# Twelve load slots and one form of matmul per product in the experts of a first layer

## What is computed

```python
def expert_choice_ffn(h, router, w_gate, w_up, w_down):
    cap = CAPACITY_FACTOR * t // N_EXPERTS            # 64 of 512 tokens, 32 of 256 context rows
    aff = softmax(h @ router)
    gates, idx = lax.top_k(swapaxes(aff, 1, 2), cap)  # 16 experts
    xs = h[idx]
    a = einsum('becd,edf->becf', xs, w_gate)          # 1024 x 1024 per expert
    u = einsum('becd,edf->becf', xs, w_up)
    y = einsum('becf,efd->becd', silu(a) * u, w_down)
    return zeros.at[idx].add(y * gates)

x_new = x_new + g2 * expert_choice_ffn(h2, ...)
if need_ctx:                                          # first layer only
    xc = xc + cg2 * expert_choice_ffn(hc2, ...)
```

## Time and profile before

| | us |
|---|---|
| median of 3 runs (2745.11 to 2752.82) | 2745.65 |
| the profiled execution | 2749.64 |
| its span from first to last instruction | 2747.8 |
| granted TensorE clock, mean of the span | 0.973 |

### The profile page before, as it was taken

How to read it: one execution, slowest core, us unless ns; L and a number is a source line. 1 busy time by engine, 2 the same in 40 slices (tenths; PEclk the granted TensorE clock), 3 DMA queues, 4 the chain that set the end, 5 groups by cost and what they waited for, 6 DMA issues and landing times.

```text
span 2747.8 us, 35463 instructions
## 1 busy us (share of the span) xinstructions
PE 2540.7 (92%) x13952; PEld 1520.0 (55%) x13952; DVE 1313.6 (48%) x2565; ACT 1002.7 (36%) x1859; POOL 355.3 (13%) x190
## 2 busy tenths in 40 slices
PE   6999988899999998796869999998899898999998
PEld 3875566432222322684654433442667787788887
DVE  2497544344444444577542333333754654442342
ACT  4216642244344443526523222222344334322222
POOL 0220002001111111220010000000223221122221
PEclk9999999899999999999989999999999899999999
DMA  6216733599999998320039999998121002222221
GB/s 255 66 62 241 281 123 123 218 359 375 365 355 371 370 361 332 127 92 1 16 146 372 421 421 421 421 421 352 47 77 32 15 13 96 94 92 98 92 85 54
DMA packets 85452, 567.72 MB, mean 207 GB/s; under 512 B 11744, under 2 KB 12000, under 8 KB 20264
## 3 DMA queue, kind: packets, MB, share of 16 engines
q1 hardware_dynamic: 79128, 547.01, 51.0%
q0 software_dynamic: 3616, 11.80, 1.9%
q10 hardware_dynamic: 2544, 6.66, 0.7%
HBM read 550.74 MB, written 14.68 MB: 206 GB/s over the span
## 4 chain that ended last, share of the span: by engine, by line
PE 46%; DVE 3%; DMA 1%; ACT 1%; issue 1%; ACTq 0%; DVEq 0%
PE PS L1024 11%; PE PS L1124 4%; PE PS L1122 4%; PE PS L1123 4%; PE PS L1136 3%; PE PS L1137 3%; PE PS L1138 3%; PE PS L1082 2%; PE PS L1112 2%; PE PS L795 1%; PE PS L1248 1%; DMA X<-in_w_up_dram 1%; PE PS L1253 1%; PE PS L1168 1%; PE PS L1154 1%
## 5 line engine op out<-in xcount | busy, mean ns | idle before, releaser
L2646 POOL TENSOR_TENSOR WHL<-RING,WHL 128x1024 fp32r<-128x1024 f32 x64 | 172.7, 2698 | 1489.4 <-ACT WHL L1369 1489.4
L1024 PE MATMUL PS<-RING,RF 128*64 128x512 f32 x1208 | 284.6, 603 | 4.0 <-DVE AR L2303 1.4
L1024 PE MATMUL PS<-WIDE,RF 128*64 128x512 f32 x1168 | 269.5, 597 | 0.0
L1369 ACT ACTIVATE WHL<-RING 128x1024 fp32r<-128x1024 f32 x129 | 134.5, 1047 | 213.1 <-PE PS L1138 129.4
L1122 PE MATMUL PS<-RR,WHL 128*128 128x512 f32 x512 | 205.0, 400 | 1.8 <-DVE RR L2399 1.8
L1124 PE MATMUL PS<-RR,WHL 128*128 128x512 f32 x512 | 203.2, 397 | 0.0
L1123 PE MATMUL PS<-RR,WHL 128*128 128x512 f32 x512 | 201.6, 394 | 0.0
L1024 PEld LDWEIGHTS PS<-RING,RF 128*64 128x64 f32 x1208 | 78.9, 137 | 181.6 <-issue 172.7
L1024 PEld LDWEIGHTS PS<-WIDE,RF 128*64 128x64 f32 x1168 | 79.2, 136 | 166.8 <-issue 155.5
L1877 DVE TENSOR_TENSOR WHL<-RING,WHL 128x1024 fp32r<-128x1024 f32 x65 | 79.5, 1224 | 172.3 <-ACT WHL L1369 166.1
L1624 ACT ACTIVATE RF<-PS,MODS,MSC 128x128 f32<-128x128 f32 x192 | 74.4, 438 | 231.0 <-PE PS L1082 129.9
(11 more groups left out here) (386 smaller groups left out, 4931.5 us busy)
## 6 DMA issues: line engine op xcount, KB each, us to landing
RING<-in_w_gate_dram SPq DMA_DIRECT2D x75, 1024.0 KB, 7.5
WIDE<-in_w_down_dram SPq DMA_DIRECT2D x69, 1024.0 KB, 7.8
RING<-in_w_up_dram SPq DMA_DIRECT2D x61, 1024.0 KB, 5.7
RING<-in_ada_w_dram SPq DMA_DIRECT2D x48, 1024.0 KB, 6.4
WIDE<-in_w_up_dram SPq DMA_DIRECT2D x45, 1024.0 KB, 8.3
RING<-in_w_down_dram SPq DMA_DIRECT2D x38, 1024.0 KB, 8.1
WIDE<-in_w_gate_dram SPq DMA_DIRECT2D x32, 1024.0 KB, 8.8
RING<-in_w_in_dram SPq DMA_DIRECT2D x30, 1024.0 KB, 5.0
```

The costliest lines, as they stand in the source:

```text
L1024: ins = e.matmul(a[r:r + 64, :], xs[:, j, 0:64], w[:, i, :], start=j < 2, stop=j > 5)
L1369: e.activation(h, load_buffer(ld)[:, js, cs], ACT.Copy).then_inc(act, A(("hi", st["i"])))
L2646: e.tensor_tensor(lo, load_buffer(loads[st["load"]])[:, js, cs], h.bitcast(F32), ALU.subtract).then_inc(pool, G(("lo", st["i"])))
```

## The change

In the first layer's experts twelve slots take the place of six. Added are slot 3, a part of RF (slot 8), two parts of AR that held HN (9 and 11), and the two pairs of token tiles of X (12 and 13). The rows of X and HN are written to DRAM ahead of slot 3's first load in that layer, and slots that lie in X, AR or RF wait for what was there before. `product` on TensorE now takes both loads of a product: one form on both in the first half, the other form on both in the second, and the form changes its place from product to product, so that a product begins with the form in which the one before ended. A product's two loads are released in its second half. In the first layer the pump runs twice in the first half of a product and not in the second, where it ran once in each; between `index` and the first `pick` lie eight pumps in place of four. One scratch buffer moves from RF to AR. The second layer keeps its order.

```diff
-                wide = len(loads) - 4
+                wide = len(loads) - (4 if l else 5)
         for ld in loads[wide:]:
-            ld["slots"] = (7, 8, 9, 4, 5, 6, 10, 0, 1, 2, 3) if l else (4, 5, 6, 0, 1, 2)
-        for ld in loads[wide - 4:]:
+            ld["slots"] = (7, 8, 9, 4, 5, 6, 10, 0, 1, 2, 3) if l else (4, 5, 6, 8, 3, 12, 13, 9, 11, 1, 2, 0)
+        for ld in loads[wide - (4 if l else 3):]:
             ld["expert"] = True
...
-                wide = st["i"] if k in (4, 5, 6) else wide
+                wide = st["i"] if k in (4, 5, 6) or "expert" in ld and layer == 0 else wide
...
-    next(ld for ld in loads if "expert" in ld and ld["before"] and "expert" in ld["before"])["rows"] = True
-    next(ld for ld in loads if ld["slot"] == NRING)["sums"] = True
+    next(ld for ld in loads if ld["slot"] == NRING)["rows"] = True
+    next(ld for ld in loads if ld["slot"] == NRING and ld["lead"][0])["sums"] = True
...
             plan.append(("index", g))
-            for _ in range(4):
+            for _ in range(8):
                 yield
...
-        for _ in range(1 if need_ctx else (0, 2)[q]):
+        for _ in range((2, 0)[q] if need_ctx else (0, 2)[q]):
             pump()
...
-        CD, CE = [rf(8704, 512), rf(9216, 512)], [rf(9728, 512), rf(10240, 512)]
+        CD, CE = [rf(8704, 512), rf(9216, 512)], [rf(9728, 512), ar(10688, 512)]
...
+                if "fresh" in ld:
+                    layer = ld["fresh"]
+                    if layer == 0 and ld["slot"] in (3, 12, 13):
+                        e.wait_ge(sums_out, 16 * 6)
+                    elif layer == 0 and ld["slot"] in (9, 11):
+                        e.wait_ge(rows_out, 16 * 6)
+                        e.wait_ge(pe, P["pick", 0, 0, 7])
+                    elif layer == 0:
+                        e.wait_ge(pe, P["pv", 0, 47])
...
+                def product(a, b, xs, q, *names):
+
+                    if q == 0:
+                        pair.clear()
+                        turn.append(tokens if len(turn) % 2 or not need_ctx else context)
+                        for n in range(2 if need_ctx else 1):
+                            pair.append(weights())
+                            st, w, _ = pair[n]
+                            ins = turn[-1](a if turn[-1] is tokens else b, xs, st, w, n == 0, n == 1)
+                        if not need_ctx:
+                            ins.then_inc(pe, P(("w", st["i"])))
+                    elif need_ctx:
+                        other = context if turn[-1] is tokens else tokens
+                        for n in (1, 0):
+                            st, w, _ = pair[n]
+                            other(a if other is tokens else b, xs, st, w, n == 1, n == 0
+                                  ).then_inc(pe, P(("w", st["i"]), *(names if n == 0 else ())))
```

More of the change, by code:

```diff
@@ L181, in weight_steps @@
     q, last_q, nq, wide, split = -1, {}, 0, None, None
+    layer, fresh = None, set()
     for ld in loads:
@@ L186, in weight_steps @@
         ld.update(slot=k, n=count[k], before=last.get(k), after=split if k in (4, 5, 6, 10) else None)
+        layer = ld["lead"][0] if "expert" in ld else layer
+        if k >= NRING and (k, layer) not in fresh and not k in (4, 5, 6, 10):
+            fresh.add((k, layer))
+            ld["fresh"] = layer
         last[k] = ld
@@ L573, in program @@
         rows_in, mask_in, bias_in = sem("rows_in"), sem("mask_in"), [sem(f"bias_in{i}") for i in range(2)]
-        weights_in = [sem(f"weights_in{i}") for i in range(NRING + 8)]
+        weights_in = [sem(f"weights_in{i}") for i in range(NRING + 11)]
         P, A, V, G = Done(pe), Done(act), Done(dve), Done(pool)
@@ L606, in landing @@
             else:
-                b = (rf(8192, 2048), rf(10240, 2048), ar(4096, 2048), rf(6144, 2048))[ld["slot"] - NRING - 4]
+                b = (rf(8192, 2048), rf(10240, 2048), ar(4096, 2048), rf(6144, 2048), ar(2048, 2048),
+                     *(X[:, t:t + 2, :].rearrange("p a b -> p (a b)") for t in (0, 2)))[ld["slot"] - NRING - 4]
             return b[:, 0:ld["nj"] * ld["cw"]]
@@ L745, in sync @@
                         e.dma_start(X[:, t, :], XROWS[128 * t:128 * t + 128, :]).then_inc(sums_in[t], 16)
+                    e.wait_ge(dve, V["hn", "1a", 5])
                 if "scratch" in ld:
@@ L757, in sync @@
                             e.wait_ge(dve, V["lo", st["i"]])
[L758 to L761, removed]
+                if "fresh" in ld:
[7 more added lines that the diff above has]
+                        e.wait_ge(pe, P["pv", 0, 47])
+                    elif ld["slot"] != NRING:
+                        e.wait_ge(pe, P["pv", 1, 31])
                 e.dma_start(landing(ld), in_dram(ld)).then_inc(weights_in[ld["slot"]], 16)
@@ L1018, in experts @@
                 T, n_ = (6, 96) if need_ctx else (4, 64)
[L1020 to L1033, removed]
+                pair, turn = [], []
@@ new lines, in tokens, with context @@
+                def tokens(a, xs, st, w, begin, end):
+                    for i in range(4):
+                        j, r = st["k0"] + i, 64 * (i % 2)
+                        ins = e.matmul(a[r:r + 64, :], xs[:, j, 0:64], w[:, i, :], start=begin and i < 2, stop=end and i > 1)
+                    return ins
+                def context(b, xs, st, w, begin, end):
+                    for i in range(4):
+                        j, r = st["k0"] + i, 32 * i
+                        ins = e.matmul(b[r:r + 32, :], xs[:, j, 64:96], w[:, i, :], start=begin, stop=end)
+                    return ins
@@ new lines, in product @@
+                def product(a, b, xs, q, *names):
[14 more added lines that the diff above has]
+                                  ).then_inc(pe, P(("w", st["i"]), *(names if n == 0 else ())))
+                    else:
+                        st, w, _ = weights()
+                        tokens(a, xs, st, w, False, True).then_inc(pe, P(("w", st["i"]), *names))
@@ L1045, in experts @@
                                 e.wait_ge(act, A["pick", l, ex // 2, 7])
-                        st, wt, _ = weights()
-                        product(*up, picked_tokens(ex // 2, n_)[:, :, ex % 2, :], st, wt
-                                ).then_inc(pe, P(("w", st["i"]), ("upq", l, ex, half, w, q)))
+                        product(*up, picked_tokens(ex // 2, n_)[:, :, ex % 2, :], q, ("upq", l, ex, half, w, 1))
                     elif what == "flip":
@@ L1062, in experts @@
                                 e.wait_ge(act, A["flip", l, ex, 1])
-                        st, wt, _ = weights()
-                        product(*down, hidden(ex, n_), st, wt).then_inc(pe, P(("w", st["i"]), ("downq", l, ex, half, q)))
+                        product(*down, hidden(ex, n_), q, ("downq", l, ex, half, 1))
                     elif what == "pick":
```

## The result

The changed kernel takes 2732.31 us (median of 7 runs, 2730.24 to 2737.22) against 2751.0 for the kernel before in the same comparison (7 runs, 2745.11 to 2753.78): 18.7 us less, a ratio of 0.994 with a 95% interval of 0.9923 to 0.9957. The forecast was 18.4 us less, and 2727 in absolute time; the time is 5 us above that because the kernel before has its median 5.3 us above the 2745.65 from which the forecast was worked out.

What follows compares the result with a forecast made beforehand. TensorE was taken as the bound, with the loads following it. Terms: -19.4 - 7.3 + 6.9 + 1.4 = -18.4 us, from a median of 2745.65 to 2727 us; own range 2720 to 2734, with rivals 2717 to 2738.

Steps and rivals of the forecast that it cites:

- Change of form: TensorE, first layer's experts: 113 stretches of one matmul form instead of 242, 0.15 us each, gain 19.4 us.
- Gather: Token-row gather between index and first pick: more time ends TensorE's waits, gain 7.3 us (5.7 and 1.6 of slow clock).
- First pair: Start of expert 2: forced picks make TensorE wait for ACT's copies, loss 6.9 us (5.3 and 1.6 of slow clock).
- Spreads: First products: spreads placed in pairs wait 3.4 us against 2.0, loss 1.4 us.
- Slots and loads: Expert weight loads: 10 in at the start instead of 3, no cost; 19 us in hand, 2 without seven further loads.
- That the early losses are hidden: Rival, first pair and spreads: ACT and DVE come in a kinder order, 26.7 us gained, 2719; chance 0.12.
- That the DMA engines set the pace: Rival, experts' loads: deeper queues drop DMA to 357 GB/s, only 8.5 us gained, 2737; chance 0.09.
- The slow rival: First layer's experts: the gather queues behind weight loads and lands late, 39 us more, 2766; chance 0.04.
- The tail of the layer: After the first layer's last expert product (scatter, reload of X, norm): waits for the same things, no change.

Runs made afterwards that it cites:

- e11: The changed kernel with the old order of forms, each load done with both forms before the next; 3.1 us less than the kernel before.
- e3: The changed kernel with context first and tokens second in every product, so the form also changes between products; 6.0 us less than the kernel before.
- e9: e6 with an expert's flip placed between the two forms of the next product instead of between products; 31.6 us less than the kernel before.
- e7: The changed kernel with four steps instead of eight between index and first pick for all pairs; 0.7 us less than the kernel before.
- e5: The changed kernel with six slots and the rows written where they were before; 6.1 us less than the kernel before.
- e1: The kernel before with only the new order of forms; six slots, rows, pump and four steps stay; 4.6 us less than the kernel before.
- e10: e6 with eight slots in place of twelve; 28.6 us less than the kernel before.
- e6: The changed kernel with four steps for pair 1 and the spreads moved in pairs beside products 2 and 4; 28.1 us less than the kernel before.
- e2: The kernel before with only twelve slots and the early rows; old product, pump and distance; 1.7 us more than the kernel before.
- e8: The changed kernel measured once more, nothing altered; 17.9 us less than the kernel before.
- e4: The changed kernel with four steps instead of eight between index and first pick for pair 1 alone; 20.9 us less than the kernel before.

## Why the prediction was right, point by point

**Change of form.** Forecast 113 stretches and 0.15 us each, 19.4 in sum. The trace of the changed kernel has 113 (65 and 48). By its stretches (48 of 7.02, 34 of 1.85, 31 of 3.57) the two forms take 510.5 us, those of before (54 of 1.87, 69 of 3.58, 46 of 1.00, 73 of 1.85) 529.0: 18.5, or 0.144 for each of 129. e11 (0.144), e3 (0.137) and e9 (0.13) confirm size and cause. This term is shown; it was put 0.9 us too high.

**Gather.** All of the 5.7 us and the slow clock went, 7.3. But the step had only half the reason: in e7 the waits that come back for the place of the picks (9.8 us) are as long as those for the time (8.4).

**First pair.** Forecast 5.3 us of waits near 573 and 1.6 of slow clock. The timeline of the changed kernel, TensorE and ACT:

```profile
572.68 1.40 ACT L1654 ACTIVATE RF<-PS,MODS,MSC 128x128 f32<-128x128 f32 x4
...
574.14 0.44 PE L1106 MATMUL PS<-CON,AR 128*128 128x128 f32 x2 [1.79 <-ACT RF L1654]
...
575.21 1.40 ACT L1654 ACTIVATE RF<-PS,MODS,MSC 128x128 f32<-128x128 f32 x4
576.63 0.63 ACT L1642 ACTIVATE AR<-RF 32x512 f32<-32x512 f32 x1
577.29 1.40 ACT L1654 ACTIVATE RF<-PS,MODS,MSC 128x128 f32<-128x128 f32 x4
578.95 3.64 PE L1044 MATMUL PS<-X,RF 128*32 128x512 f32 x16 [4.11 <-ACT RF L1654]
582.52 4.04 PE L1038 MATMUL PS<-X,RF 128*64 128x512 f32 x16
```

1.79 + 4.11 = 5.9 us of waits, ACT's copies one after another as added up. The 16 context instructions behind them take 3.57 us in place of 1.85 at a granted clock of 0.50, which is 1.2 GHz (window 579 to 582), and the next stretch 0.4 more: 2.1. So 8.0 where 6.9 stood.

**Spreads.** Forecast 3.4 us of waits against 2.0; measured 3.3. With the slow clocks (some 1.4 after, 1.6 before) the loss is 1.1, forecast 1.4.

**Slots and loads.** Ten loads are in before the first product and TensorE waits for none, as forecast. What failed is the account behind it: "without the seven further loads it would be 2" in hand, so no wait. e5 has 8.6 us of waits, and e1, also with six slots, 2.1; e1's stage is 3.5 us longer, which gives its loads time, but whether that is the reason isn't shown. The sum over the stage takes the loads as an even stream; the waits come at single places, and most of e5's (5.5 us) long after the start, which points to how many loads can be ahead. The ten at the start aren't needed: e10 does as well with eight. (The forecast's 9 MB at 421 GB/s are 21 us, not 25; nothing hangs on it, as the queue was idle for 40.)

**Sum.** -18.5 - 7.3 + 8.0 + 1.1 = -16.7 against -17.4 in the stage, -17.3 in the span and -18.7 and -17.9 by the medians. Added up over the whole stage, from start to start and without the waits, the two forms take 531.8 us before and 512.7 after (slow clocks included), the small operations 46.5 in both, and the waits 8.4 and 10.0: -17.5, so nothing large is left out, and the 0.7 us between the two sums is mostly in how slow clocks are put down to terms. The forms were put 0.9 too high and the first pair 1.1 too low; that the medians lie within 0.5 us of the forecast is closer than its terms are, and so far luck.

**Rivals.** That the early losses are hidden fell: they came in full (e6 shows what hiding them is worth). That the DMA engines set the pace fell: e6 takes 12 us more out of the stage and they follow at 383 GB/s and a share of 1.00 without a wait, and the second layer shows 421. The Trainium skill's 358 GB/s per core (DMA: Bandwidth & Descriptors, section on where 436 GB/s comes from) doesn't hold here, with 368 GB/s in this stage before the change and 383 in e6; the measurement decides. The slow rival, the gather behind the weight loads, is half there: landing rose from 7.2 to 9.0 us, far from the 21 us at which it decides, and not with the number of slots (e2: 7.2). The eight steps took it in.

The tail of the layer, forecast as nothing, is 0.9 us longer: from the last product's end to L835, the transpose that starts the second layer, 18.3 us against 17.3 before. As a wait before L835 it is 18.2 us, where e8, the same kernel, has 17.3 and the others with the new product 16.7 to 17.6, so this is spread between executions.

## What to carry to other kernels

When a stage's bound engine pays a fixed price for every change of tile shape, count the changes in the trace, and order the work so that neighbours share the shape; put small operations of another shape where the shape changes anyway. Such a reordering pays only if what it makes later keeps up: shortening the products alone gave 4.6 of 18 us, since the gather, which doesn't get faster with the products, then came too late. Before moving small work, ask which engine copies it out and what that engine has to do at that place; and count the slots by how many loads must be ahead: here, with loads released in pairs, room for three products ahead did all that was needed, and with room for two TensorE waited.

## What I had not expected of the hardware

- Two waits of nearly the same length can cost very different amounts. Behind a wait of 1.81 us the clock fell to 0.54 for 3 us, behind one of 1.48 and one of 1.31 in the same kernel it did not. Nor does the length decide: in e1 it fell to 0.50 behind a wait of 2.12 (753.3 to 756.7) and stayed at 1.00 behind 2.54 and 2.36. The same two waits at the spreads cost 0.5 us of slow clock on tokens in the changed kernel and 3.9 in e4.
- A gather of two transfers lands in 7.2 to 7.7 us while loads of 1 MB are released one by one beside it and in 8.8 to 9.8 while they come in pairs, whether six or twelve slots are in use.
- With loads, gathers and scatters mixed, the DMA engines gave 383 GB/s at a share of 1.00, against 421 for loads alone.
